# Experts ordered on the chip by token count, the three lightest with 64 slots instead of 96

## What is computed

```
def moe_swiglu(h, w_router, b_router, w1, w3, w2):
    logits = (h @ w_router).astype(jnp.float32) + b_router.astype(jnp.float32)
    top_v, top_i = lax.top_k(logits, TOP_K)
    top_w = jax.nn.softmax(top_v, axis=-1)
    combine = jnp.sum(jax.nn.one_hot(top_i, N_EXPERTS, dtype=jnp.float32) * top_w[..., None],
                      axis=-2).astype(h.dtype)
    out = jnp.zeros_like(h)
    for e in range(N_EXPERTS):
        out = out + combine[..., e:e + 1] * swiglu(h, w1[e], w3[e], w2[e])
    return out
```

## Time and profile before

| what | value |
|---|---|
| median of 3 runs | 1854.92 us (1849.82 to 1856.96) |
| profiled execution, span | 1847.6 us |
| TensorE busy | 1822.4 us, 99% of the span |
| VectorE / ScalarE / GpSimd busy | 767.8 / 441.3 / 99.8 us |
| HBM read | 435.57 MB |

### The profile page before, as it was taken

How to read it: one execution, slowest core, us unless ns; L and a number is a source line. 1 busy time by engine, 2 the same in 40 slices (tenths; PEclk the granted TensorE clock), 3 DMA queues, 4 the chain that set the end, 5 groups by cost and what they waited for, 6 DMA issues and landing times.

```text
span 1847.6 us, 29302 instructions
## 1 busy us (share of the span) xinstructions
PE 1822.4 (99%) x12518; PEld 1113.7 (60%) x12518; DVE 767.8 (42%) x1280; ACT 441.3 (24%) x679; POOL 99.8 (5%) x127
## 2 busy tenths in 40 slices
PE   8999999999999999999999999999999999999998
PEld 5776666667788888888788994333333433333333
DVE  3783444478577646546555552020202020202022
ACT  4433333322522222224444332000000100000001
POOL 0160000011001001100400000000000000000000
PEclk9999999999999999999999999999999999999998
DMA  9422212255256546631342578999999899999991
GB/s 377 171 78 80 80 46 103 92 183 191 72 185 202 195 148 229 223 137 69 119 155 83 191 282 308 406 387 406 379 413 378 345 371 411 376 416 376 415 378 38
DMA packets 75153, 438.53 MB, mean 237 GB/s; under 512 B 9488, under 2 KB 10256, under 8 KB 45200
## 3 DMA queue, kind: packets, MB, share of 16 engines
q1 hardware_dynamic: 63360, 393.65, 55.2%
q0 software_dynamic: 11664, 43.00, 7.1%
HBM read 435.57 MB, written 1.05 MB: 236 GB/s over the span
## 4 chain that ended last, share of the span: by engine, by line
PE 94%; DVE 3%; ACT 1%; issue 1%; DMA 1%; SPq 0%; DVEq 0%; ACTq 0%
PE ps L2268 25%; PE ps L1823 13%; PE ps L1825 13%; PE ps L1824 13%; PE ps L2286 8%; PE ps L2095 7%; PE ps L2290 4%; PE ps L2044 2%; PE ps L2001 2%; PE ps L2070 1%; DVE wlo L1144 1%; PE ps L2055 1%; PE ps L2023 1%; PE ps L2009 1%; PE ps L2233 1%
## 5 line engine op out<-in xcount | busy, mean ns | idle before, releaser
L2268 PE MATMUL ps<-estage,xg 128*32 128x448 f32 (+1 forms) x4608 | 459.2, 557 | 0.0
L1823 PE MATMUL ps<-h_hi,whi 128*128 128x512 f32 (+1 forms) x960 | 367.8, 383 | 7.3 <-DVE h_lo L1186 4.0
L1825 PE MATMUL ps<-h_hi,wlo 128*128 128x512 f32 (+1 forms) x960 | 344.2, 359 | 0.0
L1824 PE MATMUL ps<-h_lo,whi 128*128 128x512 f32 (+1 forms) x960 | 344.1, 358 | 0.0
L2268 PEld LDWEIGHTS ps<-estage,xg 128*32 128x32 f32 x4608 | 148.7, 110 | 301.4 <-issue 300.4
L1677 DVE TENSOR_TENSOR eu<-et,ps 128x224 f32<-128x224 f32 (+1 forms) x72 | 24.4, 395 | 505.7 <-ACT et L1081 505.7
L1144 DVE TENSOR_TENSOR wlo<-stage,whi 128x2048 fp32r<-128x2048 f32 x79 | 183.9, 2328 | 78.1 <-ACT whi L770 78.0
L1823 PEld LDWEIGHTS ps<-h_hi,whi 128*128 128x128 f32 x960 | 181.1, 189 | 48.4 <-issue 14.8
L1824 PEld LDWEIGHTS ps<-h_lo,whi 128*128 128x128 f32 x960 | 181.3, 189 | 36.2 <-issue 10.5
L1825 PEld LDWEIGHTS ps<-h_hi,wlo 128*128 128x128 f32 x960 | 181.1, 189 | 27.3
L770 ACT ACTIVATE whi<-stage 128x2048 fp32r<-128x2048 f32 x79 | 150.8, 1909 | 157.5 <-PE ps L1825 157.4
(11 more groups left out here) (243 smaller groups left out, 1703.1 us busy)
## 6 DMA issues: line engine op xcount, KB each, us to landing
estage<-in_moe SPq DMA_DIRECT2D x152, 1024.0 KB, 7.2
estage<-in_moe SPq DMA_DIRECT2D x128, 896.0 KB, 6.5
stage<-in_split SPq DMA_DIRECT2D x79, 1024.0 KB, 5.2
gw<-in_mods POOLq DMA_DIRECT2D x80, 512.0 KB, 3.9
dw<-in_direct SPq DMA_DIRECT2D x36, 512.0 KB, 3.7
mw_a<-in_early SPq DMA_DIRECT2D x8, 512.0 KB, 8.3
mw_b<-in_early SPq DMA_DIRECT2D x8, 512.0 KB, 14.7
xT<-in_x SPq DMA_DIRECT2D x4, 512.0 KB, 6.0
```

Of the source, the lines that this page charges most:

```text
L1823: pe.matmul(out, hi, rhs_hi, start=first, stop=False)
L1824: pe.matmul(out, hi, rhs_lo, start=False, stop=False)
L1825: ins = pe.matmul(out, lo, rhs_hi, start=False, stop=last)
L2268: ins = pe.matmul(up_bank(x, c, t)[q * TOK:(q + 1) * TOK, 0:n], xg[:, x % BATCH, kk, t * TOK:(t + 1) * TOK], rows[:, q * n:(q + 1) * n], s ...
```

## The change

The program no longer takes expert x at position x. It has eight positions, of which 1, 4 and 7 have two column tiles (64 slots) and the others three (`TILES_AT`). Expert 0 stays at position 0. The others are ranked on the chip by their number of tokens: the four with most go to positions 2, 3, 5 and 6 and the three with fewest to 1, 4 and 7. VectorE works out the ranks and a permutation `r_perm`, brings places and combine weights into that order (`by_place`), and writes `order_i`, the first unit of each position's expert. SyncE reads a value of it ahead of each position's first transfer. Its loop is written out.

With two tiles, `up` and `down` do 16 records per unit instead of 24. In `down` all four column groups are then filled by 2 tiles x 2 halves in one bank, and `y_d` is one copy. The second pass is run if some position has more tokens than its slots. `last_down`, a special order of the last four units, is gone.

```
+TILES_AT = (3, 2, 3, 3, 2, 3, 3, 2)
+LARGE = [x for x in range(1, 8) if TILES_AT[x] == TILES_E]
+SMALL = [x for x in range(1, 8) if TILES_AT[x] < TILES_E]
+PLACE_OF_RANK = [0] + LARGE + SMALL
...
-            with sp.Fori(0, EXPERTS // PAIR) as e2:
...
+            for w in range(MOE_UNITS):
+                x, n, cols = unit_at(w)
+                if x == len(unit_of):
+                    sp.wait_ge(S("order_ready"), 1)
+                    unit_of.append(sp.value_load(order_i[0:1, x:x + 1], min_val=0, max_val=UNITS * (EXPERTS - 1)))
+                sp.wait_ge(S("e_used"), passed("e_used", p) + (w + 1))
+                rows = A["moe"][n:n + 1, :, 0:cols] if x == 0 else A["moe"][bass.ds(unit_of[x] + n, 1), :, 0:cols]
+                sp.dma_start(estage[:, LANDING[w % STAGE], 0:cols], rows.rearrange("a p n -> p (a n)")).then_inc(S(f"e_in{w % STAGE}"), 16)
...
-        with sp.If(most_r > SLOTS):
+        with sp.If(most_r > 0):
...
-                for t in range(TILES_E):
+                for t in range(TILES_AT[x]):
...
-                            t, f = (q, 0) if q < TILES_E else (0, 1)
...
+                            f, t = divmod(q, tiles)
+                            ins = pe.matmul(ps[3][q * TOK:(q + 1) * TOK, :], turned(c, b, t), rows[:, i * D + f * 512:i * D + f * 512 + 512],
+                                            start=(first and i == 0), stop=(last and i == 1))
+                    if tiles == TILES_E:
...
+            if TILES_AT[x] < TILES_E:
+                n = SLOTS_AT[x]
+                dve.tensor_copy(y_d[0:n, :], ps[3][n:2 * n, :]).then_inc(done, 1)
```

More of the change, by code:

```diff
@@ L122, with tiles_before, part_steps, parts_before @@
 assert PAIR * UNITS % STAGE == 0 and EXPERTS % PAIR == 0
+assert len(TILES_AT) == EXPERTS and TILES_AT[0] == TILES_E and TILES_AT[EXPERTS - 1] == 2
+assert all(n in (2, TILES_E) for n in TILES_AT)
+for _rank in range(1, EXPERTS):
+    assert PASSES * SLOTS_AT[PLACE_OF_RANK[_rank]] >= min(SEQ, 2 * SEQ // _rank)
+def tiles_before(x, c):
+    return CHUNKS * sum(TILES_AT[:x]) + c * TILES_AT[x]
+def part_steps(x):
+    return 5 if TILES_AT[x] == TILES_E else 1
+def parts_before(x):
+    return sum(part_steps(i) for i in range(x))
 def expert_steps(x):
@@ L137, with unit_at, down_unit @@
 LAST_DOWN = MOE_UNITS - len(DOWNS[-1]) // 2
-def unit_columns(w):
-    x = (w + len(DOWNS[-1]) // 2) // UNITS
+def unit_at(w):
+    x = min((w + len(DOWNS[-1]) // 2) // UNITS, EXPERTS - 1)
     for at, kind, c in expert_steps(x):
         if kind == "up" and at <= w < at + KD:
-            return QUADS * 2 * HWS[c]
-    return 2 * D
+            return x, KD * c + w - at, QUADS * 2 * HWS[c]
+        if kind == "down" and at <= w < at + len(DOWNS[c]) // 2:
+            return x - (c == CHUNKS - 1), down_unit(c) + w - at, 2 * D
+    return x, down_unit(CHUNKS - 1) + w - LAST_DOWN, 2 * D
+def down_unit(d):
+    return CHUNKS * KD + sum(len(DOWNS[c]) // 2 for c in range(d))
 def split_stream():
@@ L383, in build @@
     cond = fixed.take("cond", [P, KD, 2])
+    places = fixed.take("places", [P, 4, EXPERTS])
     mod = fixed.take("mod", [P, DEPTH, 2, MODS])
@@ L737, in experts @@
         def experts(p):
-            with sp.Fori(0, EXPERTS // PAIR) as e2:
[L740 to L745, removed]
+            unit_of = [0]
+            for w in range(MOE_UNITS):
[6 more added lines that the diff above has]
+                sp.dma_start(estage[:, LANDING[w % STAGE], 0:cols], rows.rearrange("a p n -> p (a n)")).then_inc(S(f"e_in{w % STAGE}"), 16)
         experts(0)
@@ L1070, in rows_hi @@
                     act.wait_ge(S("fx_sc"), 4 * p)
[L1071 to L1074, removed]
+                slot = w_slot[0:n, x - 1:x]
+                act.activation(y_rows[0:n, 0:2, 0:SEQ], ps[3][0:n, :].rearrange("p (a c) -> p a c", a=2), ACT.Copy, scale=slot).then_inc(S("y_hi_e"), 1)
+                act.wait_ge(S("y_d"), passed("y_d", p) + parts_before(x))
+                act.activation(y_rows[0:n, 2:4, 0:SEQ], y_d[0:n, :].rearrange("p (a c) -> p a c", a=2), ACT.Copy, scale=slot).then_inc(S("y_hi_e"), 1)
             def silu(c_, v0, x, c, upto):
@@ L1592, in most_of_all @@
         def most_of_all():
             for n in range(1, PASSES):
[L1595 to L1598, removed]
+                step(dve.scalar_tensor_tensor(posm[:, n, :, :], places[:, 2, :].unsqueeze(1).to_broadcast([P, 2, EXPERTS]), -float(n),
+                                              posm[:, 0, :, :], ALU.mult, ALU.add))
@@ new lines, in most_of_all @@
+            step(dve.tensor_copy(r_order[:, 0, :], ps[4][:, 0:EXPERTS]))
+            step(dve.tensor_copy(r_order[:, 1, :], places[:, 3, :]))
+            step(by_place(r_order[:, :, :], r_order[:, :, :]))
+            dve.tensor_copy(order_i[:, :], r_order[:, 1, :]).then_inc(S("order_ready"), 1)
+            step(dve.tensor_tensor(r_order[:, 0, :], r_order[:, 0, :], places[:, 2, :], ALU.subtract))
+            step(dve.tensor_reduce(most[:, :], r_order[:, 0, :], AX, ALU.max))
+            dve.tensor_scalar(most_i[:, :], most[:, :], 0.0, None, ALU.max).then_inc(S("most_ready"), 1)
@@ L1619, in part_rows @@
             dve.wait_ge(done, count + 5)
[L1621 to L1635, removed]
         def experts(p):
@@ L1738, in _ @@
         experts(0)
-        with dve.If(most_r[0] > SLOTS):
+        with dve.If(most_r[0] > 0):
             for p in range(1, PASSES):
@@ L2275, in turned, with down @@
                 return ehT[:, c, at:at + TOK]
-            def down(v0, w, d):
+            def down(v0, w, d, x):
+                tiles = TILES_AT[x]
                 for u in range(len(DOWNS[d]) // 2):
@@ L2366, in experts @@
             pe.wait_ge(S("ehT"), passed("ehT", p) + EXPERTS * CHUNKS)
-            last_down(CHUNKS - 1)
+            down(0, LAST_DOWN, CHUNKS - 1, EXPERTS - 1)
             pe.wait_ge(S("selT"), passed("selT", p) + 2 * BATCHES)
         def last_scatter(tag, n):
+            rows = SLOTS_AT[EXPERTS - 1]
             for k4 in range(KD // 2):
@@ L2391, in _ @@
         experts(0)
-        with pe.If(most_r[0] > SLOTS):
+        with pe.If(most_r[0] > 0):
             for p in range(1, PASSES):
@@ L2439, in _constants @@
         inv_n[:, g, :] = 1.0 / (np.minimum(t + right + 1, SEQ) - np.maximum(t - left, 0))
+    x = np.arange(EXPERTS)
+    places = [np.where(x == 0, 8 * T, EXPERTS - 1 - x), [PLACE_OF_RANK.index(n) for n in x], SLOTS_AT, UNITS * x]
     out = {
@@ L2528, in layout @@
     for x in range(EXPERTS):
[L2529 to L2536 removed]
+        for c in range(CHUNKS):
+            hw, n = HWS[c], STARTS[c]
+            up = both[:, x, :, :, n:n + QUADS * hw].reshape(2, KD, P, QUADS, hw).transpose(1, 2, 3, 0, 4)
+            moe[x * UNITS + c * KD:x * UNITS + (c + 1) * KD, :, 0:QUADS * 2 * hw] = up.reshape(KD, P, QUADS * 2 * hw)
+        for d in range(CHUNKS):
             for n, (c, b) in enumerate(DOWNS[d]):
                 rows = i["moe_w2"][0][x, STARTS[c]:STARTS[c] + QUADS * HWS[c]].reshape(QUADS, BLOCKS[c], TOK, D)[:, b]
[L2539 removed]
+                moe[x * UNITS + down_unit(d) + n // 2, :, n % 2 * D:(n % 2 + 1) * D] = rows.reshape(P, D)
     gains = np.concatenate([np.stack([i["g_norm1"], i["g_norm2"]], axis=1).reshape(2 * DEPTH, D), i["g_final"][None]], axis=0)
```

156 lines of the change are left out of this document (77 added, 79 removed).

## The result

The changed kernel takes 1778.39 us, the median of four runs (1776.35 to 1779.46). Four runs of the kernel before give 1852.37 us. The ratio is 0.9597, with a 95% interval of 0.9576 to 0.9617: 74 us, or 4%, faster. The profiled execution has a span of 1777.6 us against 1847.6.

A forecast was written before the change was run, and what follows sets the result against it. TensorE was taken to bound the expert stage, the DMA's 423 GB/s after the change. Terms -85.0 + 9.0 + 0.6 = -75.4 us turn 1854.9 into 1779.5 us; range 1769 to 1811.

The forecast's parts named there:

- The bound: Expert stage: TensorE bounds it and paces the DMA; after the change the DMA isn't idle from position 1 on.
- the limit is 423: Weight transfers: the DMA can sustain 423 GB/s, 81.8 us per expert, though a whole expert showed 395 GB/s.
- those 20 to 30 us: Earlier expert stage: stretches with the deepest DMA queue, at 423, 427 and 425 GB/s; the lowest was taken as limit.
- the two slow ones: Earlier expert stage: stretches where TensorE frees slots slowly, at 367 and 353 GB/s with DMA share 0.96 and 0.97.
- The rule of about 358 GB/s per core: HBM to SBUF: by this figure the last weights land at 1853.9 us and nothing is gained; the prediction rejected it.
- Light positions: TensorE at positions with two tiles: a third of the matmul time goes, 28.3 us each, 85.0 us for three.
- The lead of the ring: Weight ring: 11 units landed ahead cover positions 1 and 4; position 7 is four units short, 9.3 us of waiting.
- The chain on VectorE: Ahead of the first gather: seven dependent steps take 1.9 us against 0.6, costing 0.6 us (bounds 0 and 1.3).
- SyncE's loads: SyncE's queue: seven value loads ahead of transfers, put at nothing; upper bound 7 x 0.5 us.
- Waits for rows of the expert before: Scatter inside a light position: cover ahead of it shrinks from 9.0 to 6.0 us but holds; 0 us, bound 2.
- The tail: Behind the last unit: `y_d` copies 64 rows for 32 with the same columns, so nothing is added.
- The distance from span to median: Whole kernel: the median of runs stays 7.3 us above the profiled span, 1772.2 us becoming 1779.5.

The follow-up runs named there:

- lighter stream: Changed kernel whose w2 transfers bring only half of the columns from unit 56 on, TensorE's instructions the same: 1768.62 us, ratio 0.9552 to before.
- filler experiment: Changed kernel with 8 more filler matmuls right behind the last down unit, ahead of the branch over the second pass: 1785.57 us, ratio 0.9638 to before.

## Why the prediction was right, point by point

**The bound.** The step from "share 0.99 at 395 GB/s" to "the limit is 423" decided between a gain of 76 and one of 40 us, and it holds. The rate of those 20 to 30 us was kept for 550 us: 425 GB/s in every stretch from 1200 to 1745 us. That their queue was deeper stood in no row of the prediction, but the trace has it: the median time to landing is 8.4, 9.3 and 8.3 us in the three stretches and 5.8 and 6.6 in the two slow ones. (Nine tenths of DMA share begin at 1155 us in the earlier trace rows, not at 1110; nothing rests on that.) The rule of about 358 GB/s per core, which the Trainium skill's "DMA: Bandwidth & Descriptors" states in the section "Where 436 GB/s comes from", does not hold here; the measurement decides, and it is 425 to 426. The same page of the Trainium skill, in the section "Measured (HBM→SBUF, 128 partitions, SWDGE, issued from GpSimd)", gives about 358 GB/s as what each core gets when both cores of an HBM domain stream. This program runs on one core; no run here has two that stream.

**Light positions.** 28.3 us each, forecast and measured (56.6 for two, 85.0 for three with a lighter stream).

**The lead of the ring.** Forecast: nothing waited for in positions 1 and 4, 9.3 us in 7. Measured: 12.3 us, 12.0 of them in 7 (against the kernel with the lighter stream). The mechanism is shown by the three kernels that move it: with the light positions at the end 43.9 us, with those at 1, 2 and 7 20.0, with a lighter stream 0. (At 1197.79 us 41 units had landed and not 42; the 42nd came 0.8 us later.) The 3 us too little are in the rate, the term that was mis-sized: 234.9 MB in 1756.3 - 1198.0 = 558.3 us, where 555.3 were forecast, is 421 GB/s and not 423, although 425 were moved. The difference lies at the end of the stream:

```profile
1700.00:1745.00 45.00, 39.14 (x368) 12.07 (x364) 10.79 (x21) 4.10 (x8) 0.00 (x0) 1.00 1.01 425
1745.00:1750.00 5.00, 3.92 (x40) 0.98 (x36) 0.00 (x0) 0.00 (x0) 0.00 (x0) 1.00 0.81 339
1750.00:1755.00 5.00, 4.01 (x40) 0.90 (x36) 0.00 (x0) 0.00 (x0) 0.00 (x0) 1.00 0.46 192
```

From 1745 to 1755 us the 16 engines were idle for 3.7 us in the mean (0.19 x 5 + 0.54 x 5) while TensorE waited for the last units. The packed trace shows why. It has a unit's landing in sixteen parts, and a unit counts as landed with the last of them. The first and the last part lie 1.9 us apart where the backlog begins (units 60 to 69), 4.6 in its middle (unit 160) and 8.8 at the last unit, whose parts landed from 1747.4 to 1756.2 us; in the kernel before it is some 2 us, 3.0 at the last unit. Under the backlog the parts drift apart, and the last unit waits for the slowest. Which engines are slow, the trace doesn't tell.

**The chain on VectorE.** Forecast 0.6 us. The seven steps took 1110.65 to 1112.45, 1.8 us against the 1.9 of the sum, and TensorE waited for `sel` for 0.4 us. The first up unit came 0.2 us later than before, in an execution whose router was itself 0.4 us earlier: 0.6 in all.

**SyncE's loads** cost nothing that can be seen: the periods of positions 1 to 3 fit to 0.1 us. **Waits for rows of the expert before:** none of TensorE's matmuls waited; only a weight load did, three times, 2.2 us in all and 0.7 at most, in the changed kernel as in the one with the lighter stream, so the cover had indeed shrunk to almost nothing.

**The tail** was put at nothing and took 19.4 us in place of 16.9. This is the one term with a wrong reason: the prediction looked only at the copy of `y_d`, and what grew lies behind it. TensorE behind the last down unit, which ends at 1830.75 in the kernel before and at 1758.22 in the changed one (filler, then sums of squares, first before, then changed):

```profile
1831.43 1.60 PE L1884 MATMUL ps<-ident,ones 128*128 128x128 f32 x12 [0.68 <-issue]
...
1834.79 3.63 PE L1864 MATMUL ps<-ones,sq_fin 128*128 128x1 f32 x32
```

```profile
1760.15 1.60 PE L1942 MATMUL ps<-ident,ones 128*128 128x128 f32 x12 [1.93 <-issue]
...
1763.79 4.60 PE L1922 MATMUL ps<-ones,sq_fin 128*128 128x1 f32 x32
```

Two things make it up. Filler and scatter start 1.9 and 3.5 us behind the last down unit; before, it was 0.7 and 2.0. In the three kernels that wait for the last weights (the filler experiment aside) this gap is 1.6 to 1.9 us, in the four that don't, 0.7 to 1.2 us. The packets of the kind `instruction` fit both: one starts 0.8 us ahead of the end of the last down unit in the former and 1.7 us ahead of it in the latter, and TensorE goes on 2.4 to 2.9 us after that start in every kernel. So the gap looks like the fetch of the instructions behind the branch, of which the matmuls still to be done cover less when TensorE has waited for its last weights. That rests on the order of time alone.

The rest is the clock, whose mean was 0.64 from 1765 to 1770 us, while the sums of squares ran. Their 32 records took 4.6 us there and 3.6 before. In the three experiments whose TensorE didn't wait at the end (halved transfers, lights at 1 and 7, lights at 1, 2 and 7) they took 5.5, 5.6 and 4.8 us, and with seven light positions, where it waited most, 3.7, so this part is not the waiting's doing. The clock fell from 2.4 to 1.2 GHz between 6.1 and 9.2 us behind the last down unit in the eight profiled executions, 7.6 in the kernel before and 8.2 in the changed one, in no order by kernel; what sets the moment stays open.

**The distance from span to median.** I added 7.3 us to the span. For the changed kernel the profiled execution's own time is 1779.46 us, 1.9 above its span, and the median is below that. The 7.3 were not overhead: with 1.9 us added, the profiled execution of the kernel before comes to 1849.5 us, beside its shortest runs (1849.79 and 1849.82) and not its median. The span was forecast at 1772.2 and is 1777.6, 5.4 too low (stage 3.3, tail 2.5, start -0.4), and the distance was too large by as much. That the median came out within 1.1 us is luck: two errors of some 5 us cancel; the gain in the stage, 76.0 forecast and 72.7 measured, is what the argument earned.

## What to carry to other kernels

When a faster engine is fed by a stream, look for the stream's limit in the short stretches where its queue is deepest; here neither its mean rate nor its busy share showed it. Then count bytes to come divided by that limit from the moment at which the consumer gets faster; less work on the consumer beyond that end brings nothing, as four more light positions showed. A ring lends its lead once and gets it back at the difference of the two rates, so put the light pieces early and apart: bunched at the end they cost 32 us more here, and two in a row 8, with the same work.

## What the runs showed that I had not expected

The DMA's busy share was 0.96 to 0.97 at 353 and 367 GB/s and 1.01 at 425: it says that packets are under way, not that the path is full.

From 1480 to 1735 us the issuing instruction itself takes 1.6 us in the median and up to 6.2 us, where it took 0.33. It isn't the backlog alone: from 1240 to 1410 us the median time to landing is 23.9 us, nearly as long as the later 24.5, and the issue takes 0.33 us in the median and at most 4.1. Nothing was lost by it here, since the transfers ahead of it were what was waited for.

With seven light positions TensorE's clock stayed at 1.00 through the nearly 500 us in which it waited before most units, at 80% busy. The start of the program, not touched by the change, differs by up to 6.5 us between executions: the kernel with the lighter stream had a clock of 0.86 in its first 50 us, the changed kernel 0.97. That is some 11 us more at 1.2 GHz and would cost 5 to 6 us, an estimate from the two means:

```profile
0.00:50.00 50.00, 40.39 (x244) 29.77 (x245) 17.11 (x34) 18.76 (x28) 0.20 (x4) 0.86 0.90 351
```
